# Up projections of a conv feed-forward computed as seven 128-wide block products in place of eight, with the sums of weight blocks made by GpSimd

## The reference

```python
D_FF = ((8 * D_MODEL // 3 + 255) // 256) * 256          # 2816

def conv_ffn(hn, w_up, conv_w, conv_b, w_down):
    u = depthwise_conv_centred(hn @ w_up, conv_w, conv_b)
    gate, val = jnp.split(u, 2, axis=-1)
    return (jax.nn.gelu(gate, approximate=True) * val) @ w_down

def second_block(x, ...):
    for l in range(DEPTH_2):                             # 2 layers
        ...
        x = x + rms_norm(mixed, mix_post_g[l])
        ff = conv_ffn(rms_norm(x, ffn_pre_g[l]), w_up[l], ffn_conv_w[l], ffn_conv_b[l], w_down[l])
        x = x + rms_norm(ff, ffn_post_g[l])
    return x
```

## Time and profile before

| | |
|---|---|
| median of 3 runs | 2045.03 us (2043.11 to 2045.64) |
| the profiled execution | 2044.89 us |
| its span in the trace | 2043.2 us |
| TensorE busy | 1953.8 us (96% of the span) |
| VectorE, ScalarE, GpSimd busy | 652.7, 411.7, 110.3 us |
| granted TensorE clock, mean | 0.989 |

### The profile page before, as it was taken

How to read it: one execution, slowest core, us unless ns; L and a number is a source line. 1 busy time by engine, 2 the same in 40 slices (tenths; PEclk the granted TensorE clock), 3 DMA queues, 4 the chain that set the end, 5 groups by cost and what they waited for, 6 DMA issues and landing times.

```text
span 2043.2 us, 23068 instructions
## 1 busy us (share of the span) xinstructions
PE 1953.8 (96%) x9008; PEld 1117.3 (55%) x9008; DVE 652.7 (32%) x1324; ACT 411.7 (20%) x871; POOL 110.3 (5%) x183
## 2 busy tenths in 40 slices
PE   7999999999989899989899999999999999999998
PEld 3767875333333233333333333756888456768863
DVE  1487513222112122211212221543333445433353
ACT  2134213111111011111101112143221023421210
POOL 0000000000000000000000000110000011000000
PEclk9999999999999999999999999999999999999999
DMA  9855368999999999999999999153544434344440
GB/s 344 295 202 191 131 231 333 418 427 428 428 427 428 428 428 427 428 428 427 428 428 428 427 426 369 62 206 114 174 137 164 147 131 165 113 135 154 136 173 33
DMA packets 136421, 582.21 MB, mean 285 GB/s; under 512 B 9848, under 2 KB 56064, under 8 KB 110752
## 3 DMA queue, kind: packets, MB, share of 16 engines
q1 hardware_dynamic: 131808, 574.70, 70.7%
q0 software_dynamic: 4544, 6.57, 1.1%
HBM read 580.18 MB, written 2.63 MB: 285 GB/s over the span
## 4 chain that ended last, share of the span: by engine, by line
PE 75%; DMA 20%; DVE 3%; ACT 1%; issue 1%; SPq 0%; DVEq 0%; ACTq 0%
PE psum L358 51%; DMA ring<-w_gu 11%; PE psum L694 11%; PE psum L636 9%; DMA work<-w_gu 9%; PE psum L2213 1%; DVE work L1854 1%; PE psum L681 1%; PE psum L670 1%; PE psum L1078 1%; DMA ring<-w_ada 0%; PE psum L1120 0%; PE psum L1109 0%; SPq L461 0%; DVE work L1852 0%
## 5 line engine op out<-in xcount | busy, mean ns | idle before, releaser
L358 PE MATMUL psum<-normed,ring 128*128 128x256 f32 (+1 forms) x2400 | 497.1, 368 | 0.0
L358 PEld LDWEIGHTS psum<-normed,ring 128*128 128x128 f32 x2400 | 434.4, 190 | 58.3 <-issue 4.1
L636 PE MATMUL psum<-ring,normed 128*64 128x512 f32 x1024 | 236.3, 615 | 33.0 <-DMA ring<-w_gu 31.8
L636 PE MATMUL psum<-work,normed 128*64 128x512 f32 x1024 | 234.3, 612 | 29.3 <-DMA work<-w_gu 29.3
L358 PE MATMUL psum<-work 128*128 128x128 f32 (+7 forms) x1248 | 227.3, 352 | 1.9 <-ACT work L2554 1.7
L358 PEld LDWEIGHTS psum<-work 128*128 128x128 f32 (+2 forms) x1248 | 151.7, 185 | 87.3 <-issue 74.3
L358 PE MATMUL psum<-ring,work 128*128 128x512 f32 (+1 forms) x464 | 197.5, 578 | 0.1
L636 PEld LDWEIGHTS psum<-ring,normed 128*64 128x64 f32 x1024 | 76.0, 141 | 190.9 <-issue 164.3
L636 PEld LDWEIGHTS psum<-work,normed 128*64 128x64 f32 x1024 | 80.5, 141 | 181.1 <-issue 181.1
L358 PE MATMUL psum<-ring,normed 128*128 128x512 f32 (+1 forms) x368 | 152.3, 567 | 0.7 <-PE psum L358 0.4
L358 PEld LDWEIGHTS psum<-ring,work 128*128 128x128 f32 x464 | 87.4, 190 | 100.0 <-issue 98.7
(11 more groups left out here) (328 smaller groups left out, 1425.0 us busy)
## 6 DMA issues: line engine op xcount, KB each, us to landing
ring<-w_gu SPq DMA_DIRECT2D x64, 2048.0 KB, 27.3
work<-w_gu SPq DMA_DIRECT2D x62, 2048.0 KB, 27.3
work<-w_dn SPq DMA_DIRECT2D x32, 2048.0 KB, 27.2
ring<-w_dn SPq DMA_DIRECT2D x28, 2048.0 KB, 27.5
ring<-w_in SPq DMA_DIRECT2D x23, 2048.0 KB, 10.1
ring<-w_up SPq DMA_DIRECT2D x44, 1024.0 KB, 7.2
ring<-w_down SPq DMA_DIRECT2D x10, 2048.0 KB, 7.8
ring<-w_ada SPq DMA_DIRECT2D x8, 2048.0 KB, 9.0
```

What stands on the lines that cost most here:

```text
L358: return pe.matmul(out, lhsT, rhs, start=first, stop=last, **kw)
L636: ins = pe.matmul(b[r], self.hgT[:, 2 * q + k, r], ws[e][:, k, n0:n0 + 512], start=q == 0 and k == 0, stop=q == QUARTERS - 1 and k == 1, s ...
```

## The change

In chunks 2 to 21 the product of `w_up` and `h` is taken apart into 2x2 blocks: the stationary side in (gate, value) by (even, odd feature block), the moving side in (even, odd feature block) by (first, second 128 tokens). For each of four pairs of feature blocks, seven products 128 tokens wide take the place of four products 256 tokens wide. They go to two banks, `up` and `upb`. Sums of blocks are needed on both sides:

- **x_sums**, the sums of `h`, four VectorE operations a layer.
- **u_sums**, the sums of weight blocks, four GpSimd operations 128x512 per chunk, in two buffers by turns; one of the four overwrites a block of the weights in its slot. GpSimd may start on chunk `c` when TensorE has finished chunk `c - 2`, and TensorE may start on chunk `c` when GpSimd has finished its sums.
- **first_product** on ScalarE and **up_totals** on VectorE put the seven products together in `u_out` (SBUF, two buffers); the taps are then read from there and no longer from PSUM.

The two groups of token sums for the down projection now stand in GpSimd's program right behind the weight sums of chunks 12 and 20.

```diff
@@ layer_banks @@
-    u += [("up", l, c) for c in range(2, FC)]
+    u += [(name, l, c) for c in range(2, FC) for name in ("upb", "up")]
@@ second_block @@
+    x_sums = Arena(mem.work, xn_at).take(4, KC // 2, P)
+    u_sums = [Arena(mem.work, at).take(4, P) for at in (aqk_at + 4096, aqk_at + 4608, hid_at + FC * L, ex_at + 1536, ex_at + 2048, ex_at + 2560)]
+    u_sums = [u_sums[0:3], u_sums[3:6]]
+    u_out = [hm.rearrange("p t h n -> p (t h) n"), mem.gain.rearrange("p (a b) -> p a b", b=P)]
@@ gpsimd @@
-            if l + 1 < LAYERS:
-                pool.wait_ge(gain_used, (2 * l + 1) * 2)
-                gain_rows(l + 1, 0)
-            for g in range(SEVENS // 4):
+            def chunk_sums(g):
+
                 pool.wait_ge(hid_ready, l * FC + 8 * g + 8)
...
                 step(pool.tensor_tensor(s2, s1, a11, ALU.subtract))
                 pool.tensor_tensor(s4, a12, s2, ALU.subtract).then_inc(s_ready, 1)
+
+            for c in range(2, FC):
+                if c == 2:
+                    pool.wait_ge(*B.ready("O", l, 1))
+                elif c >= 4:
+                    pool.wait_ge(*B.ready("up", l, c - 2))
+                if c == 5 and l + 1 < LAYERS:
+                    pool.wait_ge(gain_used, (2 * l + 1) * 2)
+                    gain_rows(l + 1, 0)
+                if c % 2 == 0:
+                    pool.wait_ge(*S.ready("up", l, c // 2))
+                w = slot(S.no(("up", l, c // 2)), KC, 512).rearrange("p (i k) n -> p i k n", k=2)
+                a11, a12, a21, a22 = (w[:, :, k, 256 * part + P * (c % 2):256 * part + P * (c % 2) + P] for part in range(2) for k in range(2))
+                s1, s2, s4 = u_sums[c % 2]
+                step(pool.tensor_tensor(s1, a21, a22, ALU.add))
+                step(pool.tensor_tensor(a21, a11, a21, ALU.subtract))
+                step(pool.tensor_tensor(s2, s1, a11, ALU.subtract))
+                pool.tensor_tensor(s4, a12, s2, ALU.subtract).then_inc(rope_ready, 1)
+                if c in (12, 20):
+                    chunk_sums((c - 12) // 8)
@@ tensor @@
+        def up_sevens(l, c, w):
...
+            pe.wait_ge(*up_sums_done(l, c))
+            if c == 2:
+                pe.wait_ge(s_ready, l * DOWN_SUMS + 1)
+            empty(*b)
+            empty(*a)
+            for i in range(KC // 2):
+                k, k1 = 2 * i, 2 * i + 1
+                last = i == KC // 2 - 1
+                product(b, 2, w[:, k, val], x3[:, i], i, True)
+                product(b, 1, s1[:, i], x1[:, i], i)
+                ins = product(b, 0, w[:, k1, val], x4[:, i], i)
+                if last:
+                    ins.then_inc(*B.fills(*b))
+                product(a, 1, s2[:, i], x2[:, i], i, True)
+                product(a, 3, s4[:, i], h[:, k1, P:], i)
+                product(a, 0, w[:, k, gate], h[:, k, 0:P], i)
+                ins = product(a, 2, w[:, k1, gate], h[:, k1, 0:P], i)
+            ins.then_inc(*B.fills(*a))
@@ up @@
-                empty("up", l, c)
-                for part in range(2):
-                    ins = up_part(l, c, part, slice(0, L), range(KC), w)
-                ins.then_inc(*B.fills("up", l, c))
+                up_sevens(l, c, w)
@@ scalar, tap @@
-                act.wait_ge(*B.ready("up", l, c))
+                if c < 2:
+                    act.wait_ge(*B.ready("up", l, c))
+                else:
+                    act.wait_ge(*B.released("up", l, c))
+                    act.wait_ge(*B.released("upb", l, c))
...
+            def first_product(c):
+
+                act.wait_ge(*B.ready("up", l, c))
+                act.activation(u_out[c % 2][:, 7], bank("up", l, c)[:, 0:P], ACT.Copy).then_inc(tap_ready, 1)
...
             for c in range(FC):
+                if c >= 2:
+                    first_product(c)
+                    gelu(c - 2)
                 tap(c)
-                if c >= 1:
-                    gelu(c - 1)
+            gelu(FC - 2)
             gelu(FC - 1)
@@ vector @@
+            def up_totals(c):
+
+                filled("upb", l, c)
+                dve.wait_ge(*taps_of(l, c, True))
+                v, a, b = u_out[c % 2], cut(bank("up", l, c), 4), cut(bank("upb", l, c), 4)
+                twice = lambda n: across(v[:, n], 2)
+                step(TT(v[:, 0:2], a[:, 1:3], twice(7), ALU.add))
+                step(TT(v[:, 3:5], b[:, 1:3], twice(0), ALU.add))
+                take(TT(v[:, 2], a[:, 3], v[:, 3], ALU.add), "up", l, c)
+                take(TT(v[:, 5:7], b[:, 0:2], twice(4), ALU.add), "upb", l, c)
...
-            for c in range(FC):
-                outer_taps(c)
-                if c >= 1:
-                    hidden(c - 1)
+            for c in range(FC + 2):
+                if 2 <= c < FC:
+                    up_totals(c)
+                if 1 <= c <= FC:
+                    outer_taps(c - 1)
+                if c >= 2:
+                    hidden(c - 2)
                 if c in (FC - 2, FC - 1):
                     weight_sums(c - (FC - 2))
-            hidden(FC - 1)
```

More of the change, by code:

```diff
@@ L2113, in bank, with up_of, rope_done, up_sums_done @@
         return psum[:, B.no(name)]
-    kinds = ("mix", "down")
+    def up_of(l, c, part):
+        if c < 2:
+            return bank("up", l, c)[:, part * L:(part + 1) * L]
+        return u_out[c % 2].rearrange("p a b -> p (a b)")[:, P + 4 * P * part:P + 4 * P * part + L]
+    def rope_done(l, n):
+        return rope_ready, l * (2 * NT + FC - 2) + n
+    def up_sums_done(l, c):
+        return rope_done(l, 2 * NT + c - 1)
+    def taps_of(l, c, first=False):
+        return tap_ready, l * (2 * FC - 2) + (c + 1 if c < 2 else 2 * c - (1 if first else 0))
     def sync(sp):
@@ L2396, in up_part, with product @@
             return ins
+        def up_sevens(l, c, w):
+            a, b = ("up", l, c), ("upb", l, c)
+            s1, s2, s4 = u_sums[c % 2]
+            x1, x2, x3, x4 = (x_sums[:, n] for n in range(4))
+            gate, val = slice(P * (c % 2), P * (c % 2) + P), slice(256 + P * (c % 2), 256 + P * (c % 2) + P)
+            def product(name, n, lhsT, rhs, i, fresh=False):
+                return pe.matmul(bank(*name)[:, n * P:(n + 1) * P], lhsT, rhs, start=fresh and i == 0, stop=i == KC // 2 - 1,
+                                 skip_group_check=True)
+            pe.wait_ge(*up_sums_done(l, c))
[16 more added lines that the diff above has]
+            ins.then_inc(*B.fills(*a))
         def up(l):
@@ L2953, in outer_taps @@
                         step(ins)
[L2954 removed]
+                if c < 2:
+                    take(ins, "up", l, c)
+                else:
+                    step(ins)
                 dve.nop().then_inc(conv2_ready, 1)
+            def up_totals(c):
[7 more added lines that the diff above has]
+                take(TT(v[:, 5:7], b[:, 0:2], twice(4), ALU.add), "upb", l, c)
             def hidden(c):
```

22 lines of the change are left out of this document (15 added, 7 removed).

## The result

The changed kernel takes 2057.77 us (median of 4 runs, 2057.21 to 2058.6) against 2045.34 us for the kernel before (4 runs, 2043.11 to 2045.71). The ratio is 1.0063, with a 95% interval of 1.0046 to 1.0081: 12.4 us slower. The forecast was 2038.7, faster. The profiled execution took 2058.05 us, its span being 2056.3.

A forecast was written before the change was run, and what follows sets the result against it. The prediction took TensorE, unbroken through the feed-forwards, as the bound. Products -26.4, waits behind token sums +15 and lower clock +5 gave -6.4 us, a median of about 2038.7; own case 2033 to 2043, range reaching to 2088.

The forecast's parts named there:

- A chunk costs 56 x 0.1116 = 6.25 us: TensorE's products in the rewritten chunks: 0.66 us less a chunk, 26.4 us saved over 40 chunks.
- Rival 3: Narrow products on TensorE cost more, 0.119 us a record, giving 2055 us; chance 0.05.
- A set is ready 5.4 us after TensorE has finished chunk c - 2 ... it hides: GpSimd's weight sums for a chunk hide under one chunk of TensorE's products, with 0.85 us to spare.
- VectorE and ScalarE ... Sum 4.3 us, under 6.25 ... Neither is waited for by TensorE: Per rewritten chunk VectorE needs 4.3 us and ScalarE under 2, so neither delays TensorE.
- rival 1: VectorE and GpSimd obstruct each other in SBUF during the rewritten chunks: 2087 to 2106 us, taken as 2085; chance 0.30.
- deciding point: A set of GpSimd's weight sums taking 6.3 us, not 5.4, each held up by 0.22 us, cancels the 6.4 us gain.
- VectorE is late but GpSimd loses little, and the time stays within 3 us of my forecast: The case where VectorE and GpSimd hold each other up only in the middle of an operation.
- It waits 3.7 us at the start of chunk 13: TensorE waits for weight sums behind token sums, likewise at chunk 21; four waits in two layers, 15 us lost.
- 5 us lost: Lower clock behind TensorE's four waits, three in four costing 1.7 us; 0 and 7 as the ends.
- rival 2: TensorE's waits cost no clock: 2033.6 us, the fast end of the prediction's own case.
- I cost it at nothing: VectorE's lateness of about 4 us at the loop's end, before the down projection's weight sums: at most 0.5 us a layer.
- Rival 4: Several small delays, GpSimd held up by tenths or a late down projection start, use up the gain: 2041 to 2050; chance 0.10.

The follow-up runs named there:

- e5: e4 with chunks 20 and 21 computed the old way, by sixteen products of 256 tokens: 2022.22 us, ratio to the kernel before 0.9888.
- e2: The changed kernel with GpSimd's four weight sums a chunk replaced by nine writes of a constant that read nothing: 2039.32 us.
- e3: The changed kernel with the totals written back into their PSUM banks and the outer taps reading them there: 2060.48 us.
- e9: e5 with the totals back in SBUF and the outer taps reading them there: 2044.94 us.
- after: The changed kernel itself, as the experiments call it: 2057.77 us, ratio to the kernel before 1.0063.
- e7: The kernel before with four GpSimd additions a chunk, in chunks 2 to 21, that read a constant tile and that nobody waits for: 2048.25 us.
- e10: e5 with the first group of token sums back behind the weight sums of chunk 12: 2034.13 us.
- e1: The changed kernel with both groups of token sums moved behind the weight sums of chunk 21: 2060.42 us.
- e4: e3 with the edit of e1, so totals in PSUM and token sums behind the weight sums of chunk 21: 2043.38 us.
- e8: e2 with the edit of e1, so constant writes for weight sums and token sums behind chunk 21: 2032.24 us.

## Why the prediction failed

**"A chunk costs 56 x 0.1116 = 6.25 us" was right.** Chunks without a wait take 6.25 to 6.26 us, and e5 gives the saving back in the end time. Rival 3 fell.

**"A set is ready 5.4 us after TensorE has finished chunk c - 2 ... it hides" was right.** Even at 1.33 us an operation a set takes 5.6 us, under 6.25, and only one wait of 0.38 us shows outside chunks 13 and 21. That one is the small load at chunk 5, of which the prediction said that it "fits".

**"VectorE and ScalarE ... Sum 4.3 us, under 6.25 ... Neither is waited for by TensorE" is the step that failed.** The durations came from rows in which GpSimd was idle or VectorE read PSUM. With two inputs in SBUF beside GpSimd's additions, five of the nine operations take up to 1.4 us, and VectorE needs up to 7.9 us a chunk; it is busy for 128 us of the twenty chunks and not for 86. e2 (no reads on GpSimd) and e3 (taps from PSUM) each bring the taps back to 483 ns, and e9 prices the meeting of the taps at 22.7 us by itself. e2, where it is all but gone, lies 18.5 us under after; the forecast had missed by 19.1.

The mechanism is that of rival 1, and its size and its victim were wrong there. The rival let the two take whole turns, 1.27 + 0.483 = 1.75 us a pair, and priced TensorE by GpSimd's delay. The pair takes 1.41 us, since VectorE's operation is nearly done when GpSimd's next one starts; GpSimd is hardly slower and TensorE does not wait for it in every chunk. Its deciding point, 0.22 us on each of the four weight sums (0.25 by its own 6.41 us a chunk), was never reached (0.06 in the mean), and the change was slower all the same. The sign that the prediction named for this rival, outer taps longer than 0.48 us, did appear. The prediction had this case in one sentence, "VectorE is late but GpSimd loses little, and the time stays within 3 us of my forecast"; that sentence overlooked that the token sums, which stand in front of weight sums, need VectorE's `hid`.

The Trainium skill, SBUF — State Buffer, "Who interferes with whom", says that a VectorE instruction with two SBUF inputs contends with a GpSimd instruction that reads SBUF, and not with one that only writes. The traces agree on both halves, 1.38 us beside L2210 and 0.48 beside the writes in e2. They agree too that one SBUF input is outside it (483 ns in e3 and e7, 425 for L3048). The prediction took more from it, that the first one holds the ports for all of its time, and so whole turns of 1.75 us. Here page and measurement differ: a pair takes 1.41 us, since GpSimd's next addition starts 0.2 us before VectorE's operation ends (1496.49 and 1496.69), and the measurement decides. How unequal the loss is, 0.9 us on one side and 0.06 on the other, the traces alone tell.

**"It waits 3.7 us at the start of chunk 13" was right without the meeting** (3.25 in e2, 3.93 in e3 and e10) and too small with it (6.0 to 7.4), since the lateness of `hid` is added. **"5 us lost" to the clock** was too small a term: 10.4 us measured. It was sized on waits of 2.8 us, of which only some cost clock (the prediction counted seven of thirteen; the trace has a fourteenth, at 699.26, with 7.09 us, so it is seven of fourteen). Every wait of 3.9 us or more had a clock of 0.50 behind it, in after and in the experiments. So rival 2 fell, and four waits cost 2.0 to 3.0 us each, where the prediction took three at 1.7.

**The start of the down projection, "I cost it at nothing"**, held in after, and for the reason given there, the wait at chunk 21. It hid what the stage needs of VectorE. Each kernel that took the wait away and left VectorE with the stage's load (e1, e4, e8, e9) paid 3.9 to 11.9 us of waiting a layer there, clock apart (e8 and e1 at the ends). Rival 4, small delays in this place, did not happen in after.

In one line: forecast -26.4 + 15 + 5 = -6.4; measured in the profiled execution -26.4 + 26.4 + 10.4 = +10.4. Its span is 13.1 us longer, so about 1 us in the two feed-forwards and 1.8 us outside them stay without a row. By the medians the change costs 12.4 us.

## What to carry to other kernels

When work goes to GpSimd beside VectorE, look up for each VectorE operation in that stretch whether both tensor inputs are in SBUF, and price it at the length of GpSimd's operation; leaving one input in PSUM took that price away here. When a wait is to be taken away, ask which engine uses it to catch up: e1, e3 and e4 each removed a real cost and found it again a stage later. The gain came only when both causes and the next stage's load were dealt with together (e5, 1.1% faster than before).

## What the runs showed of the hardware that I had not expected

- The loss from the meeting is unequal for outer taps: VectorE 0.48 to 1.37 us, GpSimd 1.27 to 1.33. For weight sums beside token sums it is less so: VectorE 0.69 to 1.64, GpSimd 1.27 to 1.59 (e4, and the same in e7).
- What the clock costs behind a wait of TensorE hardly grows with the wait: 1.5 to 3.1 us in the traces behind one of 3.9 (e3, e8, e10), 1.6 and 3.1 behind 7.1 (e9), 2.0 to 3.0 behind 6.0 to 7.4 (after). Several short waits can so cost more clock than a few long ones (13.8 us in e3, 10.3 in after). Behind 3.25 us (e2) three of four waits had it.
- A product 128 columns wide costs little over half of one of 256 (0.1116 and 0.2158 us a record), also where three sources and seven PSUM regions alternate.
